# RWKV pair loop of a two-layer encoder: front work spread over two steps, one factor by 32x32 transposes, eight conditioning steps moved

## The chip, the cores and the metric

The kernel is written instruction by instruction for one core of a Trainium2 chip. Each engine (TensorE = PE, VectorE = DVE, ScalarE = ACT, GpSimd = POOL, SyncE = SP) runs its own list of instructions in order, and an instruction may wait for semaphores that others raise. The metric is the device time of one execution in microseconds; of several runs the median is given.

## What is computed

The reference is a two-layer encoder on a sequence of 256 tokens of width 2048, in fp32. Every sub-layer is `x <- LayerNorm(alpha*x + (1+gate) * f(x*(1+scale)+shift))`, with shift, scale and gate from a conditioning vector c. Layer 0 mixes tokens with a bidirectional RWKV-7 scan (16 heads of 64) beside gated linear attention (GLA, 4 heads); layer 1 with differential attention; each layer has a SwiGLU FFN behind it. The change is in the RWKV part and in where layer 0's conditioning is computed:

```
def _ada(c, w, b):                       # shift, scale, gate of one sub-layer
    mod = silu(c) @ w + b
def step(S, inp):                        # RWKV-7, forward and backward in time
    r_t, w_t, k_t, v_t, kk_t, a_t = inp
    sa = -einsum('dbhvk,dbhk->dbhv', S, kk_t)
    S = (S * w_t[..., None, :] + sa[..., :, None] * (kk_t * a_t)[..., None, :]
         + v_t[..., :, None] * k_t[..., None, :])
    return S, einsum('dbhvk,dbhk->dbhv', S, r_t)
```

with `kk = l2norm(k * k_k)`, `k = k * (1 + (a-1) * k_a)`, `w = exp(-0.607 * sigmoid(...))`, and to the output of the scan a normalisation per head, a bonus `sum(r*k*r_k) * v` and a gate g.

## The kernel before

The matrix products with large weights run as three fp32r matmuls for each tile (high and low parts). The RWKV scan between the input projection and the output projection is done in chunks of 64 tokens: 4 chunks, 2 directions, so 8 units of 64x64 for each head; two heads make a pair (one on partitions 0 to 63, one on 64 to 127), and there are 8 pairs. Inside a chunk the recurrence is a triangular system, and its inverse is built up in levels: blocks of 1, 2, 4, ... 32 columns are merged. The kernel holds it twice, as V and as its transpose W. At level lv the PE forms `L1 = GA^T V` (`level_q`, 16 matmuls of 64x64, two for each unit), the DVE masks it to Q, the PE forms `V += W^T Q` in bank L2 (`level_v`) and `W += Q^T W` in bank L3 (`level_w`), and ACT copies both banks to R_V and R_W. At level 5 only W is formed, and copied to R_WF.

A loop over t runs from -2 to 8 and works on three pairs at a time:

- levels of pair t (`lev`): five `level_q`, four `level_v`, five `level_w`; the second half of its masked scores (`scores(t,2)`, `scores(t,3)`); transposes of its factors (`turn_ab`, `turn_v`);
- chain of pair c = t-1 (`chain`): for chunk i the PE does `chain_x`, ACT copies R_X, the PE does `chain_u` (L2361 for all of these), ACT copies R_U (L1489), the PE does `chain_s`, the DVE updates the state (`state`, L1949, L1952); then `outputs(c)`, its moments on the DVE, the normalisation a step later;
- front of pair n = t+1 (`front`): the token shift (`shifts`, `mix`), running sums of the decay (`sums`), the norm of k (`square` on ACT, `head_sums` on the PE, `clamp` on the DVE, then `norm_ln` L1439 and `norm_exp` L1444 on ACT, each behind a table load), `exps` (L1453), `keys`, `unit_keys` (L1894 to L1899, which raises q_ready), `factors` (L1909 to L1915), then `scores(n,0)`, `scores(n,1)`, their masks (L1924) and `first(n)` (L1930, L1935 on the DVE, then on the PE 16 transposes into L2 and 16 copies into L3) with which the levels start, and `bonus(n)` (L2558). The z columns of pair t+2 are turned (`z_turn`, L2378) and multiplied for the decays (`up_decays`, L2387) at the end of the step.

The order is written out by hand, as one loop body for each engine; nothing reorders it. Steps t = -2 and -1 fill this pipeline, step 7 also begins GLA (`gla = t == PAIRS - 1`), and step 8 has pair 7's chain beside GLA.

The conditioning of a part is 16 steps `cond_step(u)` of the DVE, each a multiply-add over 128x2048 (L526) of a 1 MB piece of ada_w that SP has fetched to one of two slots of adaw. Units u = 32 to 47 run in the loop, two in each of the steps 0 to 7, and SP fetches them in a loop of its own ahead of the weights of the output projection. GLA uses the same slots for its own work after that. The output projection has 16 units (q, s): for each, ACT rounds 1 MB of weights (`high`), the DVE takes the remainder (`low`, L479), the PE does 24 matmuls; at s = 2 of q = 1, 2, 3 the DVE also does `end_block`.

Of the kernel before, what the change touches and what calls it, by code (L numbers as in the profile page):

```python
# [14 lines left out]
P = 128  # L15
# [4 lines left out]
W = 512  # L20
# [82 lines left out]
def build_trunk(nc, x_in, c_in, ada_w, ada_b, ln_g, ln_b, ffn_w_in, ffn_w_out, ab_w_in, ab_w_out,  # L103
# [3 lines left out]
    with ExitStack() as ctx:  # L107
# [59 lines left out]
        R_v = sb("R_v", [P, 2, SEQ], stack=r2)  # L167
        R_sq = sb("R_sq", [P, SEQ], stack=r2)
# [24 lines left out]
        R_bonus = sb("R_bonus", [P, 3, SEQ], stack=r2)  # L193
        R_g = sb("R_g", [P, 4, SEQ], stack=r2)
        R_dec = sb("R_dec", [P, 3, NCH, 2], stack=r2)
# [105 lines left out]
        JOBS = (0, 1, 4, 5)  # L301
        FIRST_JOBS = len(JOBS) + 1
# [63 lines left out]
        wc_ready = sem("wc_ready")  # L366
# [856 lines left out]
        def _(sp):  # L1223
# [23 lines left out]
            for u in range(32, 48):  # L1247
                if u == 45:
# [100 lines left out]
        def _(act):  # L1349
# [69 lines left out]
            def rates(n):  # L1419
# [4 lines left out]
                if n > 3:  # L1424
                    act.wait_ge(tail_done, n - 3)
                act.activation(R_lw[:, 2], P1[:, 0:SEQ], ACT.Sigmoid, bias=tab[:, T_A0 + n:T_A0 + n + 1])
                act.activation(R_g[:, n % 4], P1[:, SEQ:W], ACT.Copy).then_inc(up_act, 1)

            def square(n):
# [4 lines left out]
                act.activation(R_sq[:], R_rk[:, 1], ACT.Square, scale=neg[:, n:n + 1]).then_inc(sq_ready, 1)  # L1434
# [11 lines left out]
            def exps(n):  # L1446
# [4 lines left out]
                if n > 2:  # L1451
                    act.wait_ge(s_ready, 3 * (n - 2))
# [3 lines left out]
                act.activation(R_dec[:, n % 3, :, 0], e1_at[:, 0, :, CH - 1], ACT.Copy)  # L1456
                act.activation(R_dec[:, n % 3, ::-1, 1], e1_at[:, 1, :, 0], ACT.Copy).then_inc(exps_ready, 1)
# [18 lines left out]
            def level_w(t, lv):  # L1476

                act.wait_ge(w_done, 5 * t + lv)
                act.activation(flat(R_WF if lv == LEVELS - 1 else R_W), L3, ACT.Copy).then_inc(wc_ready, 1)
# [81 lines left out]
            for t in range(-2, PAIRS + 1):  # L1561
                c, n, m = t - 1, t + 1, t + 2
                lev, chain, front = 0 <= t < PAIRS, 0 <= c < PAIRS, 0 <= n < PAIRS
                if chain:
                    chain_x(c, 0)
                if t == PAIRS - 1:
                    gla_gate_act()
# [9 lines left out]
                if front:  # L1577
                    rates(n)
                    if m < PAIRS:
                        load_up(m)  # L1580
                if lev:
                    level_w(t, 1)
                if t == PAIRS - 1:
                    out_gate(0)
                if front:
                    square(n)
# [6 lines left out]
                if t == PAIRS - 1:  # L1593
                    out_gate(1)
                if t == PAIRS:
                    gla_exps(1)
                if lev:
                    level_w(t, 2)
                if front:
                    norm_ln(n)  # L1600
                if chain:
                    chain_x(c, 2)
                if lev:
# [5 lines left out]
                if front:  # L1609
                    norm_exp(n)  # L1610
                if lev:
                    level_w(t, 3)
                if t == PAIRS - 1:
                    gla_exp(0)
                    gla_exp(1)
                if front:
                    exps(n)
                if chain:
                    chain_x(c, 3)
                if lev and t < PAIRS - 1:  # L1620
                    turned_ab(t, 0)
                if lev:
                    level_v(t, 4)
                if t == PAIRS - 1:
# [4 lines left out]
                if lev and t < PAIRS - 1:  # L1629
                    turned_ab(t, 1)  # L1630
                if lev:
                    level_w(t, 4)
                if t == PAIRS - 1:
                    turned_ab(t, 0)
                if lev:
                    turned_v(t)
                if t == PAIRS - 1:
                    turned_ab(t, 1)
                if lev:
                    level_w(t, 5)  # L1640
                if t == PAIRS - 1:
# [3 lines left out]
                if t == PAIRS:  # L1645
                    gla_exps(2)
                if chain:
# [3 lines left out]
                if m < PAIRS:  # L1651
                    z_copy(m)
                if front:
                    level_v(n, 0)
                if m < PAIRS:
                    z_own(m)
                    decays(m)
# [132 lines left out]
        def _(dve):  # L1790
# [66 lines left out]
            def mix(n):  # L1857
# [3 lines left out]
                if n > 1:  # L1861
                    dve.wait_ge(v_turned, n - 1)
                for j in (1, 0, 2):
                    o = R_rk[:, j] if j < 2 else R_v[:, n % 2]
# [62 lines left out]
            def first(n):  # L1927
# [5 lines left out]
                if n:  # L1933
                    dve.wait_ge(w_done, 5 * n)
                dve.tensor_tensor(R_W[:], R_C0[:], eye2.unsqueeze(1).to_broadcast((P, NU, CH)), ALU.add).then_inc(first_ready, 1)  # L1935
# [6 lines left out]

            def state(c, i):

                dec = R_dec[:, c % 3, i].unsqueeze(2).to_broadcast((P, 2, CH))
# [8 lines left out]
            def bonus(n):  # L1954

                dve.wait_ge(bonus_done, n + 1)
                dve.tensor_tensor(R_bonus[:, n % 3], C2[:, SEQ:W], R_v[:, n % 2], ALU.mult).then_inc(bonus_out, 1)
# [955 lines left out]
```

## Time and profile before

| what | us |
|---|---|
| median of 3 runs (2801.75 to 2805.22) | 2802.12 |
| the profiled execution, whole | 2806.61 |
| its span | 2804.8 |
| PE busy over the span | 2638.8 (94%) |
| DVE / ACT busy over the span | 1978.6 (71%) / 1149.2 (41%) |
| loop from the first z_turn (t = -2) to the end of step 6 | 387.76 to 638.92 |
| step 7 and step 8 with the rest of GLA | 638.92 to 733.55 |

The span is the profiled execution's from first to last instruction. A "step" of the loop is counted from the first matmul of its `level_q(t,1)` to that of the next. Steps 1 to 5 repeat with 33.1 to 33.4 us each; the one shown in the rows is t = 4, at 539.85 to 573.22. A busy time of the PE counts the length of each matmul, and these overlap; what a block of matmuls costs is the distance from its start to the start of the next block, when nothing waits between them.

### The profile page before, as it was taken

What the parts mean: (1) busy time and instruction counts of PE and PEld (TensorE: products, weight loads), DVE (VectorE), ACT (ScalarE), POOL (GpSimd) and SP (SyncE); (2) the same over time, 40 slices, a digit from 0 to 9 for tenths busy, and PEclk for the clock granted to TensorE, in tenths of its full rate; (3) what the DMA queues carried; (4) which work ended last, traced back from release to release, by engine and by line L of the source; (5) the groups of instructions that cost most, each with busy time, mean ns of one, the idle gap of its engine ahead of it and who ended that gap; (6) DMA issues with size and microseconds to landing.
All of it is one profiled execution on the core that took longest, in us unless ns stands there. A gap on an engine that the chain in (4) does not pass through costs nothing. (4 is left out here: it accounts for less than half of the span.)

```text
span 2804.8 us, 42833 instructions
## 1 busy us (share of the span) xinstructions
PE 2638.8 (94%) x18094; PEld 2197.3 (78%) x18094; DVE 1978.6 (71%) x1855; ACT 1149.2 (41%) x1319; POOL 283.8 (10%) x199
## 2 busy tenths in 40 slices
PE   1999979998899999999999899999999999999996
PEld 1888869997777888888888677888778888888885
DVE  6778956776566878888888778865668755555557
ACT  1443335555434333333333345546443333333332
POOL 0000000000004000000000086541040000000000
PEclk9999989999999999999999899999999999999998
DMA  9999912220546888888888467744568755555552
GB/s 352 330 337 368 372 65 72 72 68 32 210 152 240 328 298 329 302 327 303 325 307 323 134 211 251 271 155 140 189 222 316 270 185 191 194 186 188 194 189 81
DMA packets 252890, 636.73 MB, mean 227 GB/s; under 512 B 10222, under 2 KB 17060, under 8 KB 230596
## 3 DMA queue, kind: packets, MB, share of 16 engines
q1 hardware_dynamic: 246578, 621.84, 62.2%
q10 hardware_dynamic: 6162, 12.72, 1.2%
q8 instruction: 115, 1.88, 0.3%
q14 instruction: 35, 0.29, 0.0%
HBM read 632.42 MB, written 2.10 MB: 226 GB/s over the span
## 5 line engine op out<-in xcount | busy, mean ns | idle before, releaser
L479 DVE TENSOR_TENSOR s_wl<-s_raw,s_wh 128x2048 fp32r<-128x2048 f32 x393 | 913.7, 2325 | 509.4 <-ACT s_wh L474 501.1
L474 ACT ACTIVATE s_wh<-s_raw 128x2048 fp32r<-128x2048 f32 x396 | 758.3, 1915 | 1163.6 <-PE pa L639 503.0
L637 PE MATMUL pa<-s_wh,s_hth 128*128 128x512 f32 x1616 | 646.0, 400 | 17.2 <-DVE s_wl L479 11.4
L639 PE MATMUL pa<-s_wh,s_htl 128*128 128x512 f32 x1616 | 635.0, 393 | 0.0
L638 PE MATMUL pa<-s_wl,s_hth 128*128 128x512 f32 x1616 | 634.6, 393 | 0.0
L637 PEld LDWEIGHTS pa<-s_wh,s_hth 128*128 128x128 f32 x1616 | 307.0, 190 | 92.6 <-DVE s_wl L479 16.1
L639 PEld LDWEIGHTS pa<-s_wh,s_htl 128*128 128x128 f32 x1616 | 306.6, 190 | 65.5
L526 DVE SCALAR_TENSOR_TENSOR s_wide<-s_adaw,s_silu_c,s_wide 128x2048 f32<-128x2048 f32 x150 | 351.8, 2346 | 6.4 <-DMA s_adaw<-in_ada_w 6.4
L638 PEld LDWEIGHTS pa<-s_wl,s_hth 128*128 128x128 f32 x1616 | 307.1, 190 | 60.2
L637 PE MATMUL pb<-s_wh,s_hth 128*128 128x512 f32 (+1 forms) x816 | 318.9, 391 | 0.7 <-DVE s_wl L479 0.7
L639 PE MATMUL pb<-s_wh,s_htl 128*128 128x512 f32 (+1 forms) x816 | 318.6, 390 | 0.0
L638 PE MATMUL pb<-s_wl,s_hth 128*128 128x512 f32 (+1 forms) x816 | 318.6, 390 | 0.0
L637 PE MATMUL py<-s_wh,s_guh 128*128 128x512 f32 x640 | 251.2, 393 | 4.4 <-DVE s_ysum L1061 4.4
L639 PE MATMUL py<-s_wh,s_gul 128*128 128x512 f32 x640 | 249.3, 390 | 0.0
L638 PE MATMUL py<-s_wl,s_guh 128*128 128x512 f32 x640 | 249.1, 389 | 0.0
L637 PEld LDWEIGHTS pb<-s_wh,s_hth 128*128 128x128 f32 x816 | 154.0, 189 | 33.7 <-DVE s_wl L479 1.9
L639 PEld LDWEIGHTS pb<-s_wh,s_htl 128*128 128x128 f32 x816 | 154.0, 189 | 31.8
L638 PEld LDWEIGHTS pb<-s_wl,s_hth 128*128 128x128 f32 x816 | 154.0, 189 | 31.5
L876 POOL TENSOR_TENSOR s_small<-s_small 128x2 f32<-128x2 f32 x4 | 3.8, 947 | 1585.0 <-DVE s_small L865 1585.0
L1061 DVE TENSOR_TENSOR s_ysum<-s_ysum,py 128x512 f32<-128x512 f32 x172 | 116.4, 683 | 47.3 <-PE py L639 46.9
L637 PEld LDWEIGHTS py<-s_wh,s_guh 128*128 128x128 f32 x640 | 120.1, 188 | 35.2 <-DVE s_ysum L1061 7.7
L639 PEld LDWEIGHTS py<-s_wh,s_gul 128*128 128x128 f32 x640 | 120.1, 188 | 25.3
(372 smaller groups left out, 2698.2 us busy)
## 6 DMA issues: line engine op xcount, KB each, us to landing
s_raw<-in_ffn_w_in SPq DMA_DIRECT2D x176, 1024.0 KB, 5.2
s_adaw<-in_ada_w SPq DMA_DIRECT2D x160, 1024.0 KB, 6.0
s_raw<-in_ffn_w_out SPq DMA_DIRECT2D x88, 1024.0 KB, 7.5
s_raw<-in_ab_w_in SPq DMA_DIRECT2D x48, 1024.0 KB, 9.0
s_raw<-in_diff_w_in SPq DMA_DIRECT2D x48, 1024.0 KB, 5.2
s_raw<-in_ada_w SPq DMA_DIRECT2D x16, 1024.0 KB, 8.5
s_raw<-in_ab_w_out SPq DMA_DIRECT2D x16, 1024.0 KB, 5.4
s_qkv<-in_ada_w SPq DMA_DIRECT2D x16, 1024.0 KB, 7.2
```

The source lines that it names most:

```text
L474: act.activation(wh[:, s % 2, :, 0:width], raw[:, s, :, 0:width], ACT.Copy).then_inc(hi_done, 1)
L479: dve.tensor_tensor(wl[:, s % 2, :, 0:width], raw[:, s, :, 0:width], wh[:, s % 2, :, 0:width].bitcast(F32), ALU.subtract).then_inc(lo_done, 1)
L526: dve.scalar_tensor_tensor(wide[:], frm, silu_c[:, bass.ds(k, 1)], wide[:], ALU.mult, ALU.add).then_inc(ada_step, 1)
L637: pe.matmul(o, a_hi, w_hi, start=start and k == 0, stop=False)
L638: pe.matmul(o, a_hi, w_lo, start=False, stop=False)
L639: mm = pe.matmul(o, a_lo, w_hi, start=False, stop=stop and k == UK - 1)
L876: pool.tensor_tensor(small[:, 38:40], small[:, 34:36], small[:, 95:96].to_broadcast((P, NT)), ALU.pow).then_inc(end_rstd, 1)
L1061: dve.tensor_tensor(y, y, py[:, i], ALU.add).then_inc(py_free, 1)
```

## The change

- The loop runs from t = -3. The front of a pair is split: z_turn, z_copy, z_own, decays now work on pair q = t+3; up_rates, rates, shifts, mix, sums, square, head_sums, clamp, keys, norm_ln, norm_exp, exps, unit_keys, bonus on pair m = t+2 (`ahead`); factors, scores(n,0), scores(n,1), their masks, first and level_v(n,0) on n = t+1 (`front`). R_v, R_bonus, R_g and R_dec have one buffer more, and R_sq is gone (R_rn takes its place).
- `level_w` of levels 1 to 4, ACT's copies of R_W (`level_w`) and the second half of `first` are gone. In their place the DVE turns R_V to R_W in blocks of 32x32 (`level_t`, four in each step); up to level 4 the units are zero outside such blocks. Level 5 remains as `last_w`, for which ACT writes R_W into bank L3 ahead (`last_seed`).
- Units 40 to 47 of the conditioning move to eight units of the output projection (`OUT_STEPS`), DVE step and fetch both; the loop has one cond_step in each step, and SP waits for the end of GLA (`head_done`) ahead of fetch 40.

The diff, cut to this:

```diff
+        OUT_STEPS = ((1, 0), (1, 1), (1, 3), (2, 0), (2, 1), (2, 3), (3, 0), (3, 1))
...
@@ def out_sp
                     load_unit(sp, c0 + q, s, wv[s, :, :, q * W:(q + 1) * W])
+                    if (q, s) in OUT_STEPS:
+                        u = 40 + OUT_STEPS.index((q, s))
+                        if u == 40:
+                            sp.wait_ge(head_done, GH)
+                        load_part(sp, u, u % 2, parts[1, 1, u - 32])
@@ def out_dve
+                    if (q, s) in OUT_STEPS:
+                        cond_step(dve, 40 + OUT_STEPS.index((q, s)))
@@ sync
-            for u in range(32, 48):
+            for u in range(32, 40):
@@ scalar, loop
+                if ahead:
+                    norm_ln(m)
...
+                if lev and not gla:
+                    turned_v(t)
+                if lev:
+                    last_seed(t)
...
+                if front:
+                    level_v(n, 0)
+                if ahead:
+                    norm_exp(m)
                 if lev:
-                    level_w(t, 4)
...
+                    last_w(t)
...
+                if ahead:
+                    exps(m)
@@ vector
+            def level_t(t, lv):
+
+                dve.wait_ge(vc_ready, 5 * t + lv + 1)
+                dve.transpose(flat(R_W), flat(R_V)).then_inc(wt_ready, 1)
...
                 if front:
                     masked(n, 0)
                     masked(n, 1)
                     first(n)
                 if lev and not gla:
-                    cond_step(dve, 32 + 2 * t)
+                    cond_step(dve, 32 + t)
+                if lev:
+                    level_t(t, 4)
+                    level_q(t, 5)
...
+                if ahead:
+                    unit_keys(m)
+                    bonus(m)
...
-                if lev and not gla:
-                    cond_step(dve, 33 + 2 * t)
@@ tensor
                 if lev:
                     level_q(t, 5)
                 if front:
-                    scores(n, 0)
-                    scores(n, 1)
+                    first(n)
+                if chain:
+                    outputs(c)
                 if lev:
-                    level_w(t, 5)
+                    last_w(t)
...
-                if chain:
-                    outputs(c)
-                if front:
-                    bonus(n)
-                if m < PAIRS:
-                    z_turn(m)
-                    up_decays(m)
-                if front:
-                    first(n)
+                if ahead:
+                    bonus(m)
+                if q < PAIRS:
+                    z_turn(q)
+                    up_decays(q)
```

ACT, in the middle of step 3 before: the second table load (L1444) and the exponential that ends the norm of k stand behind the copy R_U of chunk 2, ahead of chunk 3's R_X.

```order
L1489 ACTIVATE s_R_U<-pb 128x2x64
L1444 ACT_TABLE_LOAD
L1444 ACTIVATE s_R_rn<-s_R_rn 128x256
L1479 ACTIVATE s_R_W<-pa 128x512
L1453 ACTIVATE s_R_e<-s_R_cs 128x8x64
L1454 ACTIVATE s_R_e<-s_R_cs 128x512
```

ACT, end of a step after: chunk 3's copies (L1498 would be R_X, L1503 is R_U), then R_VV, the seed of L3 (L1488), R_V of `first(n)`, and only then that table load (L1453).

```order
L1503 ACTIVATE s_R_U<-pb 128x128
L1478 ACTIVATE s_R_VV<-py 128x256
L1488 ACTIVATE pa<-s_R_W 128x512
L1483 ACTIVATE s_R_V<-pt 128x512
L1453 ACT_TABLE_LOAD
L1453 ACTIVATE s_R_rn<-s_R_rn 128x256
L1493 ACTIVATE s_R_WF<-pa 128x512
L1462 ACTIVATE s_R_e<-s_R_cs 128x8x64
```

The exponential has moved behind two copies that wait for the end of the step: the seed for the fourth transpose, R_V for `first(n)` on the PE.

DVE, end of step 3 before: unit_keys (L1894 to L1899) and factors come ahead of the masks of the scores; cond_step (L526) follows first.

```order
L1899 TENSOR_TENSOR s_R_qa<-s_R_kk,s_R_lw 128x256
L1909 TENSOR_TENSOR s_raw<-s_R_kk,s_R_e 128x8x64
L1910 TENSOR_TENSOR s_raw<-s_R_rk,s_R_e 128x8x64
L1913 TENSOR_TENSOR s_xt<-s_R_ks,s_R_e 128x8x64
L1915 TENSOR_TENSOR s_xt<-s_R_qa,s_R_e 128x8x64
L1940 TENSOR_TENSOR s_R_Q<-py,s_cst 128x512
L1924 TENSOR_TENSOR s_raw<-pt,s_cst 128x512
L1924 TENSOR_TENSOR s_raw<-pa,s_cst 128x512
L1930 TENSOR_TENSOR s_R_C<-s_raw,s_cst 128x512
L1935 TENSOR_TENSOR s_R_W<-s_R_C,s_cst 128x512
L526 SCALAR_TENSOR_TENSOR s_wide<-s_adaw,s_silu_c,s_wide 128x2048
L1957 TENSOR_TENSOR s_R_bonus<-pb,s_R_v 128x256
```

The same place after: masks, first, cond_step (L528), the fourth transpose (L1952), the mask of level 5 (L1946), and then unit_keys (L1902 to L1907).

```order
L1932 TENSOR_TENSOR s_raw<-pt,s_cst 128x512
L1932 TENSOR_TENSOR s_raw<-pa,s_cst 128x512
L1938 TENSOR_TENSOR s_R_C<-s_raw,s_cst 128x512
L1941 TENSOR_TENSOR s_R_C<-s_R_C,s_cst 128x512
L528 SCALAR_TENSOR_TENSOR s_wide<-s_adaw,s_silu_c,s_wide 128x2048
L1952 STREAM_TRANSPOSE s_R_W<-s_R_V 128x512
L1946 TENSOR_TENSOR s_R_Q<-py,s_cst 128x512
L1902 SCALAR_TENSOR_TENSOR s_R_kk<-s_R_rk,s_neg,s_R_rn 128x256
L1905 SCALAR_TENSOR_TENSOR s_R_rkr<-s_R_rk,s_tab,s_R_ks 128x256
L1907 TENSOR_TENSOR s_R_qa<-s_R_kk,s_R_lw 128x256
L1968 TENSOR_TENSOR s_R_bonus<-pb,s_R_v 128x256
```

The cond_step and the fourth transpose now stand between first and unit_keys, whose last instruction raises q_ready.

PE, end of step 3 before, from the last products of outputs(c) to the next step's `level_q`: bonus (L2558), z_turn, up_decays, and `first` in two halves.

```order
L2361 MATMUL pb<-s_R_S,s_raw 64x64 x2
L2558 MATMUL pb<-s_R_rkr,s_cst 128x256
L2378 MATMUL py<-s_cst,s_z 128x128 x4
L2378 MATMUL pt<-s_cst,s_z 128x128 x2
L2387 MATMUL pa<-s_raw 128x256 x2
L2361 MATMUL pt<-s_cst,s_R_W 64x64 x16
L2361 MATMUL pa<-s_R_W,s_cst 64x64 x16
L2361 MATMUL py<-s_R_V,s_raw 64x64 x16
```

After: last_w behind outputs(c), then bonus (L2570, which waits for q_ready), z_turn, up_decays, and the next `level_q`.

```order
L2373 MATMUL pb<-s_R_S,s_raw 64x64 x2
L2373 MATMUL pa<-s_R_W,s_R_Q 64x64 x16
L2570 MATMUL pb<-s_R_rkr,s_cst 128x256
L2391 MATMUL py<-s_cst,s_z 128x128 x4
L2391 MATMUL pt<-s_cst,s_z 128x128 x2
L2402 MATMUL pa<-s_raw 128x256 x2
L2373 MATMUL py<-s_R_V,s_raw 64x64 x16
```

`first` has moved ahead of outputs(c), last_w behind it, and nothing but bonus, z_turn and up_decays is left between last_w and the next step.

## Rows read from the trace of the kernel before

**Rows 1.** Page, busy time of each engine over the span

```profile
PE 2638.8 (94%) x18094; PEld 2197.3 (78%) x18094; DVE 1978.6 (71%) x1855; ACT 1149.2 (41%) x1319; POOL 283.8 (10%) x199
```

**Rows 2.** Stages: length, busy PE, PEld, DVE, ACT, POOL; PEclk, DMA share, GB/s

```profile
387.76:412.19 24.43, 14.98 (x126) 11.56 (x128) 11.58 (x21) 10.29 (x22) 0.00 (x0) 0.59 0.05 16
412.19:440.06 27.87, 26.01 (x682) 24.24 (x680) 18.05 (x30) 16.86 (x33) 0.00 (x0) 1.00 0.08 17
539.85:573.22 33.37, 32.76 (x922) 31.16 (x920) 24.58 (x51) 18.82 (x42) 3.07 (x2) 1.00 0.24 75
606.90:638.92 32.02, 31.41 (x918) 29.97 (x916) 23.23 (x50) 17.89 (x40) 1.93 (x1) 1.00 0.19 60
638.92:679.53 40.61, 34.30 (x832) 31.43 (x829) 27.55 (x44) 19.65 (x33) 3.07 (x1) 0.92 0.14 52
733.55:824.00 90.45, 88.65 (x405) 73.43 (x404) 49.03 (x39) 38.57 (x35) 0.89 (x2) 0.99 0.65 222
```

**Rows 3.** Timeline of PE in step 4: start, length, instruction, idle before

```profile
541.11 0.70 PE L2393 MATMUL py<-s_raw 96*128 96x256 f32 x2
...
542.61 1.15 PE L2361 MATMUL pt<-s_R_Q,s_R_W 64*64 64x64 f32 x32
543.59 0.40 PE L2361 MATMUL pb<-s_R_X,s_R_WF 64*64 64x64 f32 x8
543.82 1.10 PE L2361 MATMUL pa<-s_R_W,s_R_Q 64*64 64x64 f32 x32
544.75 0.29 PE L2361 MATMUL pb<-s_R_VV,s_R_AT 64*64 64x64 f32 x4
...
546.10 1.10 PE L2361 MATMUL py<-s_R_V,s_raw 64*64 64x64 f32 x32
...
564.69 1.04 PE L2361 MATMUL pa<-s_raw,s_xt 64*64 64x128 f32 x16
...
569.16 0.70 PE L2558 MATMUL pb<-s_R_rkr,s_cst 128*128 128x256 f32 x2
...
571.31 1.15 PE L2361 MATMUL pt<-s_cst,s_R_W 64*64 64x64 f32 x32
...
573.22 0.98 PE L2361 MATMUL py<-s_R_V,s_raw 64*64 64x64 f32 x28
```

**Rows 4.** Timeline of DVE in step 4

```profile
547.24 0.69 DVE L1940 TENSOR_TENSOR s_R_Q<-py,s_cst 128x512 f32<-128x512 f32 x1 [0.62 <-PE py L2361]
...
567.33 0.69 DVE L1935 TENSOR_TENSOR s_R_W<-s_R_C,s_cst 128x512 f32<-128x512 f32 x1
567.93 2.35 DVE L526 SCALAR_TENSOR_TENSOR s_wide<-s_adaw,s_silu_c,s_wide 128x2048 f32<-128x2048 f32 x1
```

**Rows 5.** Timeline of ACT in step 4

```profile
543.80 0.60 ACT L1474 ACTIVATE s_R_V<-pt 128x512 f32<-128x512 f32 x1 [0.67 <-PE pt L2361]
...
544.29 0.27 ACT L1489 ACTIVATE s_R_U<-pb 128x128 f32<-128x128 f32 x1
...
556.44 1.28 ACT L1444 ACT_TABLE_LOAD   x1
557.74 0.42 ACT L1444 ACTIVATE s_R_rn<-s_R_rn 128x256 f32<-128x256 f32 x1
```

**Rows 6.** Groups by line on DVE: the transposes of 32x32 blocks elsewhere

```profile
L559 DVE STREAM_TRANSPOSE s_qkv<-s_wide 128x1024 f32<-128x1024 f32 x4 | 4.9, 1230 | 0.0
```

**Rows 7.** Timeline of DVE while the pipeline fills

```profile
400.25 0.48 DVE L1894 SCALAR_TENSOR_TENSOR s_R_kk<-s_R_rk,s_neg,s_R_rn 128x256 f32<-128x256 f32 x1 [1.42 <-ACT s_R_rn L1444]
...
401.20 0.43 DVE L1899 TENSOR_TENSOR s_R_qa<-s_R_kk,s_R_lw 128x256 f32<-128x256 f32 x1
```

**Rows 8.** Two long waits of PE in step 8 (timeline)

```profile
707.70 1.80 PE L2627 MATMUL pt<-s_z,s_L_kdt 64*128 64x256 f32 x8 [1.92 <-ACT s_L_kdt L1532]
...
730.94 1.91 PE L2649 MATMUL pb<-s_adaw,s_L_qb 128*64 128x256 f32 x12 [2.44 <-DVEq L2049]
```

**Rows 9.** PE behind the first of them: length, busy, PEclk, DMA share, GB/s

```profile
708.00:708.50 0.50, 0.50 (x6) 0.54 0.00 0
...
711.00:711.50 0.50, 0.50 (x9) 0.54 0.00 0
```

More of the change, by code:

```diff
@@ L1474, in level_v, with last_seed, last_w @@
                 act.activation(flat(R_V), L2, ACT.Copy).then_inc(vc_ready, 1)
-            def level_w(t, lv):
-                act.wait_ge(w_done, 5 * t + lv)
-                act.activation(flat(R_WF if lv == LEVELS - 1 else R_W), L3, ACT.Copy).then_inc(wc_ready, 1)
+            def last_seed(t):
+                act.wait_ge(wt_ready, 4 * t + 4)
+                act.activation(L3, flat(R_W), ACT.Copy).then_inc(ws_ready, 1)
+            def last_w(t):
+                act.wait_ge(w_done, t + 1)
+                act.activation(flat(R_WF), L3, ACT.Copy).then_inc(wf_ready, 1)
             def chain_x(c, i):
@@ L1560, in _ @@
             load_up(0)
[L1561 to L1563 removed]
+            for t in range(-3, PAIRS + 1):
+                c, n, m, q = t - 1, t + 1, t + 2, t + 3
+                lev, chain, front, ahead = 0 <= t < PAIRS, 0 <= c < PAIRS, 0 <= n < PAIRS, 0 <= m < PAIRS
+                gla = t == PAIRS - 1
                 if chain:
                     chain_x(c, 0)
[L1566 removed]
+                if gla:
                     gla_gate_act()
@@ L2077, in _ @@
                 if front:
-                    shifts(n)
-                    mix(n)
+                    factors(n)
+                if ahead:
+                    shifts(m)
                 if chain:
                     state(c, 0)
-                if tail and not gla:
+                if lev:
+                    level_t(t, 1)
+                    level_q(t, 2)
+                if ahead:
+                    mix(m)
+                if 0 <= p and not gla:
                     normed(p)
-                if lev:
-                    level_q(t, 2)
                 if gla:
@@ L2461, in turn_v @@
                 for k in range(NCH):
-                    mm = two(unit(P1, k), R_v[:, t % 2, k * CH:(k + 1) * CH], eye2, start=(k == 0))
+                    mm = two(unit(P1, k), R_v[:, t % 3, k * CH:(k + 1) * CH], eye2, start=(k == 0))
                 mm.then_inc(v_turned, 1)
@@ L2470, in first @@
                 for u in range(NU):
-                    mm = two(unit(L2, u), R_W[:, u], eye2, start=(u == 0))
+                    mm = two(unit(L2, u), R_C0[:, u], eye2, start=(u == 0))
                 mm.then_inc(v_done, 1)
-                if n:
-                    pe.wait_ge(wc_ready, 5 * n)
-                for u in range(NU):
-                    two(unit(L3, u), eye2, R_W[:, u], start=(u == 0))
             def level_q(t, lv):
@@ L2664, in gla_turn_out @@
                 mm.then_inc(g_oT, 1)
-            for t in range(-2, PAIRS + 1):
+            for t in range(-3, PAIRS + 1):
+                c, n, m, q = t - 1, t + 1, t + 2, t + 3
+                lev, chain, front, ahead = 0 <= t < PAIRS, 0 <= c < PAIRS, 0 <= n < PAIRS, 0 <= m < PAIRS
                 gla = t == PAIRS - 1
-                c, n, m = t - 1, t + 1, t + 2
-                lev, chain, front = 0 <= t < PAIRS, 0 <= c < PAIRS, 0 <= n < PAIRS
                 if lev:
@@ L2677, in _ @@
                     gla_turn(2)
-                if front:
-                    up_rates(n)
+                if ahead:
+                    up_rates(m)
                 if lev:
@@ L2699, in _ @@
                     chain_x(c, 1)
-                if n >= 0 and not gla:
-                    head_sums(n, t - 2)
                 if lev:
@@ L2710, in _ @@
                     pe.wait_ge(g_logit, 3)
-                    head_sums(n, t - 2)
+                    head_sums(m, t - 2)
                 if chain:
                     chain_s(c, 1)
+                if m >= 0 and not gla:
+                    head_sums(m, t - 2)
                 if lev and not gla:
```

212 lines of the change are left out of this document (93 added, 119 removed).

## The prediction

> **What bounds the kernel now.** I read the engines' busy time first. TensorE works 2638.8 of 2804.8 us [rows 1], so over the whole the other engines are cover. That is an average over stages, so the windows come next [rows 2]: step 4 of the loop lasts 33.37 us with TensorE busy for 32.76, at full clock; DVE has 24.6 and ACT 18.8. In the out-projection TensorE is busy for 88.65 of 90.45 us. Only the filling of the pipeline (15.0 busy of 24.4, clock 0.59) and step 7 (34.3 of 40.6) have TensorE waiting. Third, the timelines of step 4 on three engines give what the change turns on: how far apart blocks of matmuls start, and how long a result takes on its way through DVE or ACT and back [rows 3 to 5]. The bound in the loop is TensorE's own work. The question is whether it still is once a seventh of that work is gone.
>
> **What goes from TensorE.** A level_w costs 0.93 (543.82 to 544.75 in [rows 3]); the two halves of `first` cost 1.91 (571.31 to 573.22), half of that 0.96. The step loses 4 x 0.93 + 0.96 = 4.68 us. It has 33.37 - 0.8 of waits and gaps = 32.6 of work, so 27.9 is left. Seven steps (0 to 6) lose this, step 7 loses the four level_w.
>
> **What TensorE then waits for, in a full step.** I laid the new orders of PE, ACT and DVE beside each other with the durations of before.
> - *Chain.* Between `chain_u` and `chain_s` stood a level_w, which covered ACT. From the start of chain_u (543.59) its copy R_U is ready at 544.29 + 0.27 = 544.56, with some 0.06 to start the matmuls; but ACT copies R_V first (543.80, 0.60), and chain_u is now issued right behind level_v. From level_v's start (542.61) R_V's copy comes 1.19 later, R_U's 0.49 behind that, and 0.33 ends it: chain_s starts 2.01 behind level_v, where level_v and chain_u take 0.98 + 0.23 = 1.21. That is 0.80 of wait, three times in a step: 2.4.
> - *Mask.* level_q to Q takes 1.14 (546.10 to 547.24 in [rows 3, 4]) and 0.69 more. At level 2 only 1.3 us of other work is left in between: 0.5 of wait. At the other levels scores, turn_ab and chain blocks cover it.
> - *`first`.* scores(n,1) start at 564.69, and the mask for the transposes is ready at 567.33 + 0.69 = 568.02, 3.33 later [rows 3, 4]. Before, outputs, bonus and z_turn lay in between. Now it is scores(n,1) itself (0.88) and level_q(t,5) (0.93): 1.6 of wait (3.33 + 0.06 - 1.81). The wait for factors (0.6) ahead of scores goes in return; it is in the 0.8 above.
> - *The 32x32 transposes.* No such transpose of 128x512 is in the trace. The nearest row has 128x1024 at 1.23 [rows 6], so 0.62 by proportion, and from below 0.3, from above 1.23. I take 0.69, as DVE's other operations over 128x512 take [rows 4]. Three of them lie beside chain and scores. Level_q needs R_V and not R_W; level_v needs both Q and R_W, so transposes are late only by their own length. At 1.23 each step would be 1 to 2 us longer, at 0.3 none.
> - *bonus(m).* This is the place that decides. It waits for q_ready, raised by the last of unit_keys. Those wait for norm_exp, which on ACT now stands behind last_seed and R_V of `first`; and on DVE they stand behind cond_step, the fourth transpose and Q of level 5. Count from F, the start of scores(n,1). DVE: masks and first until F + 3.24, cond_step until + 5.49 (2.25, its 2.35 less 0.1 of overlap [rows 4]), transpose until + 6.18. ACT, released by that transpose: last_seed 0.5, R_V of `first` 0.62, until + 7.30; table load 1.28 and the exponential 0.42 [rows 5], beginning at + 8.6, Q-norm ready at + 9.0; unit_keys take 1.38 with the first matmul behind them (400.25 to 401.63, [rows 7]): + 10.4, and 0.1 of semaphores, F + 10.55. TensorE: scores, level_q, the wait and 0.98 of transposes until + 4.4, outputs 2.66 (566.50 to 569.16), last_w 0.93: F + 7.96. **The wait is 2.6 us.** DVE, not the table load alone, is half of it: without cond_step in the way the wait would be near 0.4.
> - The rest (exps behind it, the copies of rates, GpSimd) has ten microseconds until it is read, and I cost it at nothing.
>
> Sum of a full step: 27.9 + 2.4 + 0.5 + 1.6 + 2.6 = **35.0 us, against 33.37: +1.6.** The busy share falls to 0.8, and the bound moves to the loop through ACT and DVE.
>
> **By stretches.** Step 0 has no chain to wait for but the bonus wait: 27.87 to 28.6, +0.7. Steps 1 to 4: +6.5. Step 5 has the bonus wait but no z_turn and up_decays any more (1.6, from 569.69 to 571.31 [rows 3]): 0. Step 6 has no `ahead`: up_rates (1.5, 541.11 to 542.61), head_sums (1.2, two blocks of 0.6) and bonus (0.53) have moved one step up, and with the 4.68 taken and some 4 of waits added 32.0 becomes 28.7: -3.3. Step 7, where TensorE waits on DVE [rows 2], has one conditioning step less (2.25) ahead of the masks of GLA, and no level_w: -4.0 for steps 7 and 8. *Filling:* the first level_q comes at 412.19 now. One more step is walked through, whose chain is norm, table load, scores of pair 0 and then that of pair 1; laid out with the durations of the filling of before, at TensorE's half clock, it comes at 424.8: **+12.6**. *Out-projection:* each unit has 90.45/16 = 5.65 us for TensorE, and DVE is busy 49.0 of 90.45; so it idles for 41, in which eight steps of 2.25 (18 us) fit, in units without an end_block: 0, with +2 as upper end. 8 MB are fetched besides, at a DMA share of 0.65. The fetches stand on SP's queue behind the weights of their unit, and the first waits there for GLA's end, with unit (1,1)'s weights behind it; GLA is over by then.
> Sum: 12.6 + 0.7 + 6.5 + 0 - 3.3 - 4.0 + 0 = **+12.5.**
>
> **The clock.** Behind two waits of TensorE in step 8, of 1.92 and 2.44 us [rows 8], the granted clock fell to 0.50, the lower of its two levels (1.2 GHz); for the first the 3.50 us that followed ran at 0.51 [rows 9], which loses 3.5 x 0.49 = 1.7 us. After waits up to 0.8 in the loop it stayed at 1.00 [rows 2]. The bonus wait of 2.6 stands in six steps (0 to 5), directly behind work at full pace. I count four falls: 4 x 1.65 = +6.6. In all 12.5 + 6.6 = +19, on the profiled 2806.6. I put it on the median, 4.5 below: 2802.1 + 19 = **2821**.
>
> ACT's table load takes 1.28 here and its exponential starts 1.30 behind the load's start [rows 5]. The Trainium skill, "ScalarE: Activation LUTs", section on what a table load costs, gives about 1283 ns and another 1380 ns of drain for each switch, 2.66 us. By the trace the second part is not there; by the page the bonus wait would be 1.4 longer in seven places, some +10 us (an estimate from the page). The row decides.
>
> **Rivals.**
> - *The clock stays.* The waits are 2.6 beside 1.6 and six of 0.8, and one wait of 1.42 in step 7 brought no fall at once. Then +12.5: 2814.6. Chance 0.20.
> - *The clock falls more often* (with `first`'s 1.6 and the bonus wait 5 us later, in all six steps, or twice), or the transposes take their upper end: 6 x 1.65 x 1.3 or 5 x 1.5 in place of 6.6, 2825 to 2831. Chance 0.20.
> - *The out-projection gets late.* If DVE's remainder of the weights waited for cond_step, up to 8 x 2.25 = 18 more, 2824 to 2839. Against it stands DVE's idle time there. Chance 0.05.
> - *No bonus wait.* If norm_exp came in time (ACT's sequence reaches it ahead of R_V of `first`, or DVE has cond_step done sooner since its slot's data is early), six waits of 2.6 go, with their clock: 2821 - 15.6 - 6.6 = 2799, which is within 0.2%. Chance 0.07.
> - *The other side: TensorE stays the bound.* Then all 4.68 comes back in seven steps (-32.8), step 7 gives 4, and the filling costs 12.6 (less if it overlaps better): -24, 2778. It decides by whether R_U's copy and the masks come within the work left: my waits of 0.8 and 1.6 would have to be covered, so ACT would have to be 0.8 faster between level_v and chain_s than in [rows 5]. Nothing speaks for it but that I may have placed the blocks wrongly. Partly so (half the waits) gives 2795. Chance 0.10, all of it faster.
>
> **How the numbers follow.** The forecast has 0.38, its own range 2810 to 2829. With the rivals above and below 2802 to 2833 leaves out 0.10 + 0.07 below and some 0.03 above. A change of 0.2%, 5.6 us, is what a measurement of this kernel can just tell from none: same is 2796.5 to 2807.7. Faster 0.10, same 0.07, slower 0.83.
>
> **What would show it.** Right: first level_q(0,1) near 425; steps 1 to 4 of 35 us; in them TensorE idle ahead of bonus (L2570) for 2.4 to 2.6 released by DVE's L1907, ahead of `first` 1.6 released by DVE's L1941, ahead of chain_s three times 0.8 released by ACT's L1503; DVE's L1952 at 0.6 to 0.7; stretches at PEclk 0.50 behind bonus; the out-projection at 90 to 92. Wrong: steps of 29 us with TensorE busy throughout; L1952 above 1 us; a clock at 1.00 through steps 1 to 5, or lower in all of them; DVE late with low in the out-projection.

## The result: 38 us slower by the medians, twice what was forecast

| | before | after |
|---|---|---|
| median of 4 runs, us | 2801.93 | 2839.70 |
| all runs, us | 2800.99 to 2805.22 | 2834.24 to 2840.53 |
| ratio | 1 | 1.0126 (95%: 1.0114 to 1.0138) |
| span of the profiled execution, us | 2804.8 | 2838.4 |

The direction was forecast, the size was not: 2821 with a range of 2802 to 2833, and 2839.7 measured. Measured again with the run wt_best below, the changed kernel gave 1.0124 (1.0109 to 1.0140). The spans of the two profiled executions lie 33.6 us apart; the working below is against that. "Lower clock" in the table is what the lower granted clock lost: for each half microsecond one minus the granted clock, times the time that TensorE was busy in it.

The stages of the kernel after, in the columns of [rows 2] (length, busy PE, PEld, DVE, ACT, POOL, then PEclk, DMA share, GB/s): filling, step 0, step 3, step 6, steps 7 and 8, and the out-projection with its end:

```profile
387.12:427.49 40.37, 25.17 (x115) 18.16 (x115) 17.90 (x34) 20.73 (x42) 0.00 (x0) 0.50 0.06 16
427.49:458.34 30.85, 24.13 (x517) 21.69 (x516) 19.62 (x33) 15.20 (x30) 0.00 (x0) 0.89 0.14 45
529.92:566.59 36.67, 30.54 (x758) 27.89 (x757) 25.02 (x54) 18.00 (x42) 2.02 (x2) 0.96 0.12 39
637.41:668.26 30.85, 26.12 (x737) 25.32 (x738) 19.15 (x41) 6.72 (x18) 1.01 (x1) 0.94 0.01 3
668.26:766.47 98.21, 76.95 (x1157) 64.03 (x1153) 62.96 (x146) 47.64 (x114) 7.39 (x9) 0.84 0.13 44
766.47:862.74 96.27, 94.37 (x422) 77.93 (x421) 69.22 (x50) 38.98 (x33) 0.89 (x2) 0.97 0.81 306
```

The kernel before in the two stages that [rows 2] cut differently (steps 7 and 8 together, out-projection with its end):

```profile
638.92:733.55 94.63, 77.63 (x1284) 64.76 (x1281) 64.03 (x136) 48.02 (x115) 9.46 (x9) 0.90 0.19 67
733.55:827.98 94.43, 92.63 (x422) 76.69 (x421) 51.10 (x42) 39.15 (x35) 0.89 (x2) 0.99 0.65 223
```

| stage | before | after | difference | lower clock, before and after | forecast, clock apart |
|---|---|---|---|---|---|
| filling (first z_turn to first level_q) | 24.4 | 40.4 | +15.9 | 5.3, 12.4 | +12.6, at half clock |
| step 0 | 27.9 | 30.9 | +3.0 | 0, 2.6 | +0.7 |
| steps 1 to 4 | 133.2 | 144.5 | +11.4 | 0, 4.2 | +6.5 |
| steps 5 and 6 | 65.7 | 65.4 | -0.3 | 0, 2.6 | -3.3 |
| steps 7 and 8 | 94.6 | 98.2 | +3.6 | 8.9, 12.6 | -4.0 |
| out-projection and its end | 94.4 | 96.3 | +1.8 | 0.9, 2.7 | 0 |
| all else | | | -1.8 | | 0 |
| sum | | | +33.6 | +15.0 without the filling | +12.5, and 6.6 of clock |

In the loop TensorE is no longer full: busy 30.5 of 36.7 us in step 3, where [rows 2] have 32.8 of 33.4. Where it waits is read from the timeline of PE (start, length, instruction, idle before and its releaser), step 3 of the kernel after:

```profile
534.84 0.33 PE L2373 MATMUL pb<-s_R_VV,s_R_AT 64*64 64x64 f32 x4 [0.72 <-ACT s_R_U L1503]
...
538.11 1.15 PE L2373 MATMUL pt<-s_R_Q,s_R_W 64*64 64x64 f32 x32 [0.32 <-DVE s_R_Q L1946]
539.09 0.40 PE L2373 MATMUL pb<-s_R_X,s_R_WF 64*64 64x64 f32 x8
540.12 0.33 PE L2373 MATMUL pb<-s_R_VV,s_R_AT 64*64 64x64 f32 x4 [0.63 <-ACT s_R_U L1503]
...
547.05 0.33 PE L2373 MATMUL pb<-s_R_VV,s_R_AT 64*64 64x64 f32 x4 [0.63 <-ACT s_R_U L1503]
...
553.34 1.13 PE L2373 MATMUL py<-s_R_V,s_raw 64*64 64x64 f32 x32
555.87 1.15 PE L2373 MATMUL pt<-s_cst,s_R_C 64*64 64x64 f32 x32 [1.41 <-DVE s_R_C L1941]
...
559.48 1.15 PE L2373 MATMUL pa<-s_R_W,s_R_Q 64*64 64x64 f32 x32
563.05 0.70 PE L2570 MATMUL pb<-s_R_rkr,s_cst 128*128 128x256 f32 x2 [2.42 <-DVE s_R_qa L1907]
```

These are the six waits of the prediction, at their places and by their releasers. The idle time printed is a little shorter than what a wait costs, since the matmul before it is drawn to its very end (0.40 where the next would start after 0.23). By starts: 540.12 - 539.09 - 0.23 = 0.80 ahead of chain_s; 555.87 - 553.34 - 0.93 = 1.60 ahead of `first`; 563.05 - 559.48 - 0.93 = 2.64 ahead of bonus. The chain behind the last is read from DVE and ACT in the same step:

```profile
555.73 2.35 DVE L528 SCALAR_TENSOR_TENSOR s_wide<-s_adaw,s_silu_c,s_wide 128x2048 f32<-128x2048 f32 x1
558.00 0.70 DVE L1952 STREAM_TRANSPOSE s_R_W<-s_R_V 128x512 f32<-128x512 f32 x1
...
561.61 0.49 DVE L1902 SCALAR_TENSOR_TENSOR s_R_kk<-s_R_rk,s_neg,s_R_rn 128x256 f32<-128x256 f32 x1 [2.34 <-ACT s_R_rn L1453]
```

```profile
558.73 0.60 ACT L1488 ACTIVATE pa<-s_R_W 128x512 f32<-128x512 f32 x1 [5.23 <-DVE s_R_W L1952]
559.27 0.58 ACT L1483 ACTIVATE s_R_V<-pt 128x512 f32<-128x512 f32 x1
559.87 1.28 ACT L1453 ACT_TABLE_LOAD   x1
561.16 0.42 ACT L1453 ACTIVATE s_R_rn<-s_R_rn 128x256 f32<-128x256 f32 x1
```

ACT stood still for 5.23 us for the fourth transpose, which stood behind the conditioning step; only then came the seed, R_V, the table load and the exponential for which unit_keys waited.

The clock, from windows of PE (length, busy, PEclk, DMA share, GB/s) at the waits for bonus that end at 527.77, 563.05 and 599.94, all 2.42 long; the first window begins inside its wait:

```profile
526.50:530.50 4.00, 2.73 (x31) 1.00 0.11 43
563.50:567.50 4.00, 4.00 (x34) 0.57 0.01 4
601.00:605.00 4.00, 4.00 (x48) 0.57 0.07 20
```

Twice the granted clock fell to its lower level (1.2 GHz), which loses 4.0 x 0.43 = 1.7 us, and once, behind the same wait, it did not. From step 0 to 6 the falls lose 9.4 us in the kernel after and nothing in the kernel before. Without them steps 1 to 4 are 34.7 to 35.2 us long, 35.1 on average where 35.0 was forecast.

### The profile page after: what moved, and what is told of

It reads as the page before. It is cut to its first block and busy times, and to the rows that moved or that the text cites. A ratio compares the mean times of both kernels' runs of the same rounds, so it can differ in the third digit from the quotient of the medians.

```text
span 2838.4 us, 40259 instructions
## 1 busy us (share of the span) xinstructions
PE 2626.9 (93%) x16814; PEld 2178.6 (77%) x16814; DVE 1998.6 (70%) x1887; ACT 1136.8 (40%) x1295; POOL 272.0 (10%) x199
## 5 line engine op out<-in xcount | busy, mean ns | idle before, releaser
L528 DVE SCALAR_TENSOR_TENSOR s_wide<-s_adaw,s_silu_c,s_wide 128x2048 f32<-128x2048 f32 x150 | 351.8, 2346 | 0.0
L639 PEld LDWEIGHTS py<-s_wh,s_guh 128*128 128x128 f32 x640 | 120.1, 188 | 35.2 <-DVE s_ysum L1070 7.7
```

What stands on the lines that cost most here:

```text
L528: dve.scalar_tensor_tensor(wide[:], frm, silu_c[:, bass.ds(k, 1)], wide[:], ALU.mult, ALU.add).then_inc(ada_step, 1)
L639: pe.matmul(o, a_hi, w_hi, start=start and k == 0, stop=False)
```

## Experiments

All ratios are to the kernel before, timed in the same rounds on the same chip.

**The moved conditioning alone (cond_only).** The kernel before with

```diff
-            for u in range(32, 48):
+            for u in range(32, 40):
...
                     load_unit(sp, c0 + q, s, wv[s, :, :, q * W:(q + 1) * W])
+                    if (q, s) in OUT_STEPS:
+                        u = 40 + OUT_STEPS.index((q, s))
+                        if u == 40:
+                            sp.wait_ge(head_done, GH)
+                        load_part(sp, u, u % 2, parts[1, 1, u - 32])
...
+                        cond_step(dve, 40 + OUT_STEPS.index((q, s)))
```

and one conditioning step in each step of the loop.

> The kernel before with one part of the change alone: conditioning units 40 to 47 computed and fetched in the output projection, one conditioning step for each step of the loop. Theory A (this part is nearly free, the loss lies in the loop's waits and in the filling): steps 0 to 5 unchanged, step 7 shorter by up to 2, the output projection longer by the 1.8 us seen in the changed kernel: 2799 to 2805. Theory B (the time beyond my forecast lies here, because DVE or the fetches are late in the output projection): 2808 to 2815.

Measured: 0.9996 (0.9987 to 1.0005). Steps 1 to 5 last 32.9 to 33.4, the out-projection and its end 93.9. (By the same rows these steps last 32.9 to 33.7 in the kernel before, not 33.1 to 33.4.) Steps 7 and 8 last 91.0 for 94.6 in these two profiles, 2.5 of that by fewer falls of the clock; in the time of all runs no gain is clear. This part costs nothing; theory B falls.

**W by transposes, without the split front (wt_cond).** The loop order of the kernel before; `level_w` 1 to 4 out on PE and ACT, `level_t` ahead of each next `level_q` on DVE, `last_seed` in the place of ACT's copy of level 4.

> The changed kernel without the front split: the loop order of the kernel before, W by 32x32 transposes, conditioning moved. Theory A (removing level_w gives TensorE time back except where it covered ACT's copy of U; the split front is what costs, by the wait ahead of bonus and a longer filling): a step loses 4.7 of work and gains about 3 of waits, no wait ahead of bonus, filling as before: 7 steps of about -1.7, 2788 to 2794. Theory B (the transposes on DVE are on the path, whatever the front does): steps as long as in the changed kernel without its bonus wait, 2802 to 2812.

Measured: 2798.1, 0.9975 (0.9965 to 0.9986), 7 us less than the kernel before. That is less than theory A gave (8 to 14), and a step shows why: 33.18 us, 0.2 less than before with 4.7 of work gone. (Steps 7 and 8 last 90.0, 4.7 less than before.) The stage, and all waits of PE in it (in total, times, longest):

```profile
536.05:569.23 33.18, 29.17 (x756) 26.91 (x756) 24.75 (x53) 17.49 (x39) 1.01 (x1) 1.00 0.13 42
```

```profile
PE pb L2373 <- ACT s_R_U L1504: 2.0, 3, 0.7
PE py L2373 <- ACT s_R_V L1484: 1.2, 2, 0.7
PE pt L2373 <- DVE s_xt L1924: 0.9, 1, 0.9
```

No engine is full: DVE has 24.8 and ACT 17.5 of 33.2. The work that was taken out had covered the time that results take through other engines. The printed waits are 4.1 in all where the step before has 0.6, and each costs a little more than is printed, so together they are about as long as the work was.

**unit_keys ahead (a_keys).** The changed kernel with

```diff
@@ ACT
+                if ahead:
+                    norm_exp(m)
                 if lev:
                     last_seed(t)
...
-                if ahead:
-                    norm_exp(m)
@@ DVE
-                if lev and not gla:
-                    cond_step(dve, 32 + t)
...
                     unit_keys(m)
+                if lev and not gla:
+                    cond_step(dve, 32 + t)
+                if ahead:
                     bonus(m)
```

> The changed kernel with two moves: on ACT norm_exp (table load and exponential) ahead of last_seed instead of behind R_V of first, on DVE the conditioning step between unit_keys and the product with bonus instead of ahead of the fourth transpose. Theory A (the wait ahead of bonus comes from that chain, and TensorE's clock falls behind it): 2.4 us less in each of steps 0 to 5 and the falls of the clock in steps 1 to 5 gone (1.7 each), 2815 to 2819. Theory B (another wait takes its place, or the clock falls for another reason): only the wait or part of it goes, 2824 to 2832.

Measured: 2819.3, 1.0049 (1.0035 to 1.0063), where the changed kernel has 1.0126 and 1.0124: 21 us less. The wait for bonus is gone and steps 1 to 5 run at full clock. The steps are 33.5 and not 32.4, because another wait has come up, 0.8 ahead of up_rates for ACT's z_own, behind exps. The first row is the whole step, the others all waits of PE in it:

```profile
514.73:548.24 33.51, 29.03 (x758) 26.84 (x757) 24.75 (x53) 17.24 (x39) 1.01 (x1) 1.00 0.14 43
```

```profile
PE pb L2374 <- ACT s_R_U L1503: 2.0, 3, 0.7
PE pt L2374 <- DVE s_R_C L1941: 1.4, 1, 1.4
PE py L2409 <- ACT s_R_zo L1415: 0.8, 1, 0.8
PE pt L2374 <- DVE s_R_Q L1946: 0.3, 1, 0.3
```

**The wait filled with work (a_fill).** Nothing gets shorter here; TensorE turns the same columns three more times while it waits; with `False` the turn raises no semaphore.

```diff
+                if lev and q < PAIRS:
+                    for extra in range(3):
+                        z_turn(q, False)
                 if ahead:
                     bonus(m)
```

> The changed kernel with three further z_turn of the coming pair in each of steps 0 to 4 ahead of bonus, whose results are overwritten by the real one: 2 us of TensorE work inside its wait of 2.4, nothing shortened. Theory A (the lower clock follows the wait): the time falls by 1.7 for each of the falls behind bonus, 4 or 5 of them, 2831 to 2834, with steps of 35.0. Theory B (the clock falls for the sum of waits in the step or something else): 2839 to 2842, the falls stay.

Measured: 2828.5, 1.0085 (1.0071 to 1.0099), 11 us less than the changed kernel with 10 us more of work for TensorE. One of its steps:

```profile
490.56:525.83 35.27, 31.26 (x776) 28.90 (x775) 24.85 (x53) 17.17 (x40) 1.02 (x1) 1.00 0.13 40
```

Steps 1 to 5 stand at PEclk 1.00 though the smaller waits are still there, so those of 0.3 to 1.4 us bring no fall there by themselves: the wait for bonus is needed. (In step 0 the fall stays, shorter, behind waits of 1.4.) That the wait for bonus is enough is not shown; a_chain below speaks against it. Steps 0 to 6 are 6.4 us shorter, 6.2 of it by the clock; in the profile the rest lies in the filling and in steps 7 and 8, which the edit does not touch and where the clock stood otherwise in this execution (37.7 for 40.4, and 94.4 for 98.2). So only some 6 of the 11 us are shown to come from the edit.

**Step 8 put back (a_step8).** Reading steps 7 and 8 after the result, I found a move that no term of my sum had. In step 8 `head_sums` (the transposes of pair 6's normalised outputs) stood ahead of chunk 1's chain_u before, behind its chain_s after. The kernel after, PE and then DVE:

```profile
715.81 0.69 PE L2373 MATMUL pb<-s_R_X,s_R_WF 64*64 64x64 f32 x8 [3.90 <-ACT s_R_X L1498]
...
717.78 1.06 PE L2373 MATMUL pa<-s_cst,s_R_yn 64*64 64x64 f32 x16
...
722.37 0.69 PE L2373 MATMUL pb<-s_R_S,s_raw 64*64 64x64 f32 x8 [3.10 <-DVE s_R_S L1963]
```

```profile
718.89 0.48 DVE L1992 SCALAR_TENSOR_TENSOR s_R_bonus<-pa,s_tab,s_R_bonus 128x256 f32<-128x256 f32 x1 [6.21 <-PE pa L2373]
...
721.67 0.28 DVE L1960 TENSOR_TENSOR s_R_S<-s_R_S,pb 128x128 f32<-128x128 f32 x1
```

DVE's `finish` waits 6.21 for those transposes, and behind it stand three products of GLA (0.69 each) and the state for which TensorE then waits 3.10. Before, they took the time in which TensorE waited for R_X anyway:

```profile
684.89 0.68 PE L2361 MATMUL pa<-s_cst,s_R_yn 64*64 64x64 f32 x16 [1.71 <-DVE s_R_yn L1974]
686.93 0.45 PE L2361 MATMUL pb<-s_R_X,s_R_WF 64*64 64x64 f32 x8 [1.36 <-ACT s_R_X L1484]
```

```diff
+                if t == PAIRS:
+                    head_sums(m, t - 2)
                 if lev:
                     level_v(t, 2)
...
-                if m >= 0 and not gla:
+                if m >= 0 and t < PAIRS - 1:
                     head_sums(m, t - 2)
```

> The changed kernel with one block of TensorE put back: in step 8 the transposes of the normalised outputs of pair 6 (head_sums) stand ahead of chunk 1's chain_u again, as before the change, instead of behind its chain_s. Theory A (this move, which no term of my sum had, makes DVE's finish wait 6.2 us and the state of chunk 1 3.1 us late): steps 7 and 8 fall from 98.2 to 93 to 95, 3 to 5 us less than the changed kernel, about 2836 where the kernel before has 2805. Theory B (steps 7 and 8 are long for the clock alone): within 1 us of the changed kernel.

Measured: 2832.6, 1.0107 (1.0089 to 1.0125), 5 us less than the changed kernel. The intervals overlap, so the time alone does not show it. The profile does: steps 7 and 8 take 89.6 us, for 98.2 and 97.5 in the two profiles of the changed kernel. Their row, and the stretch of lower clock at the place of the waits in the changed kernel (714 to 728) and in a_step8 (709 to 716):

```profile
665.21:754.78 89.57, 70.67 (x1158) 58.73 (x1154) 62.77 (x146) 47.33 (x114) 7.14 (x9) 0.94 0.14 49
```

```profile
714.00:728.00 14.00, 8.34 (x100) 0.52 0.01 1
709.00:716.00 7.00, 5.56 (x56) 0.51 0.01 2
```

Of the 8.6 us between the profiles 7.5 are lower clock (12.6 and 5.1 lost) and 1.1 is the rest; against the second profile it is 5.5 of 7.9. So the moved block costs mostly by the clock. How much of the clock belongs to the move is not settled by one profile; over all profiles, steps 7 and 8 take 94.4 to 99.8 in the five where head_sums stands late in step 8, and 89.6 to 92.7 in the six changed versions where it stands early.

**chain_u ahead of level_v (a_chain).** On PE and ACT, in steps 0 to 6:

```diff
+                if chain and t < PAIRS - 1:
+                    chain_u(c, 1)
                 if lev:
                     level_v(t, 2)
-                if chain:
+                if chain and t >= PAIRS - 1:
                     chain_u(c, 1)
```

so for all four chunks, and `scores(t, 3)` moved between chain_x(c,1) and chain_u(c,1).

> The changed kernel with chain_u ahead of level_v, on TensorE and on ACT, in steps 0 to 6, and scores(t,3) between chain_x(c,1) and chain_u(c,1) so that R_X is ready. Theory A (chain_s waits since level_w no longer covers ACT's copy of U; level_v can cover it): the three waits of 0.8 go, 2.5 in each of steps 1 to 6, -15 against the changed kernel, 2823 to 2829. Theory B (R_V and with it level_q and the transposes get late by as much): -5 at most, 2835 to 2841.

Measured: 2825.5, 1.0077 (1.0062 to 1.0092), 13 us less than the changed kernel, near theory A. None of the three waits for R_U is left. The two full steps without a fall are 33.7 and 34.3, some 1.4 and 0.8 shorter and not 2.5, because a wait comes up for `finish`, which now is late for turn_ab, and in these two steps one of 0.3 and 0.8 for R_X besides. Steps 0 to 6 are 15 us shorter, 4.4 of it by fewer falls. All six waits for bonus are still 2.42 long, and only three falls came at them (at 453.5, 488.0 and 522.0) and none in steps 3 to 6: that wait alone does not decide. The waits of PE in step 2:

```profile
PE pb L2578 <- DVE s_R_qa L1915: 2.4, 1, 2.4
PE pt L2381 <- DVE s_R_C L1949: 1.4, 1, 1.4
PE pa L2381 <- DVE s_xt L2003: 0.9, 1, 0.9
```

**All of it on the split front (best1).** a_keys, a_step8 and a_chain together; exps on ACT right behind norm_exp; outputs(c) ahead of first(n) on PE, its copy ahead of R_V on ACT.

> The changed kernel with all: norm_exp and exps ahead of last_seed on ACT, conditioning step behind unit_keys, chain_u ahead of level_v, outputs(c) ahead of first(n), output copy ahead of R_V of first, step 8 as before. Theory A (the split front pays once the waits are covered): steps of 28.6 to 29.5 in place of 33.4, filling 11 to 12 longer than before, 2778 to 2792. Theory B (DVE or ACT bound the step near 31 to 32 or the clock falls again): 2795 to 2806.

Measured: 2788.0, 0.9944 (0.9930 to 0.9959), within theory A. Steps 2 to 4 last 30.1 us, 0.6 above what was expected; the filling is still 34.8 and the whole 14 us faster than before, 50 us faster than the changed kernel.

**The same on the front of before (wt_chain, wt_best).** First wt_cond with chain_u ahead of level_v and first(n) ahead of bonus:

> W by transposes and the moved conditioning with the front of the kernel before (run wt_cond, steps of 33.18), with chain_u ahead of level_v and first(n) ahead of bonus. Theory A (what ate the 4.7 us of removed work is waits of an in-order engine that other work can cover: 2.5 for U, 0.9 for R_V of first): steps of 29.8 to 30.5, 2772 to 2782. Theory B (the front's chain through ACT and DVE to factors binds the step at 33): 2792 to 2799, TensorE waiting 3 us more for factors.

Measured: 2788.3, 0.9942 (0.9929 to 0.9955), steps of 30.5 to 31.1. That lies between the two theories, 6 us above A's range (2772 to 2782). The steps come near A's 29.8 to 30.5, and the front's chain does not bind at 33 as B had it. Its filling rose to 27.5, since first(n) now stood ahead of z_turn there too, at the lower clock. Then

```diff
@@ ACT
                 if chain:
                     chain_x(c, 0)
+                if front:
+                    decays(n)
...
                     z_own(m)
-                    decays(m)
@@ PE
-                if front:
+                if front and lev:
                     first(n)
...
                     up_decays(m)
+                if front and not lev:
+                    first(n)
```

> Run wt_chain with two moves: ACT's decays (table load and two sigmoids, 2.1 us) behind its copy of R_X of chunk 0 instead of ahead of it, and first(n) behind up_decays while the pipeline fills, as in the kernel before. Theory A (what is left in the step is ACT's order again): the wait of 0.8 ahead of chain_u(c,0) goes in six steps, the filling returns from 27.5 to 24.4: 2778 to 2783. Theory B (decays are then late for up_rates and rates): the step stays at 30.6 or grows, 2785 to 2790.

Measured: 2780.2, 0.9916 (0.9902 to 0.9929). A step, the filling, and all waits of PE in the step:

```profile
497.39:527.25 29.86, 28.43 (x757) 26.60 (x757) 24.76 (x53) 17.82 (x40) 1.01 (x1) 1.00 0.15 49
387.15:412.40 25.25, 15.30 (x94) 11.49 (x95) 11.58 (x21) 10.21 (x22) 0.00 (x0) 0.56 0.05 15
```

```profile
PE pb L2384 <- ACT s_R_X L1499: 0.7, 1, 0.7
PE py L2384 <- ACT s_R_V L1484: 0.7, 1, 0.7
```

This is the fastest version found, 24 us below the kernel before and some 59 below the changed one, as theory A had it. It has the transposes and the moved conditioning, and not the split front.

**The changed kernel again (after_again).**

> The changed kernel once more, on the chip of the next run. By the first measurement it is 1.26% longer than the kernel before: 2836 to 2842 where that has 2802 to 2805. If where TensorE's clock falls varies between executions, its runs spread by more than those of the kernel before (up to 6 us), with one fall (1.7 us) more or less at a time.

Measured: 2838.9, 1.0124 (1.0109 to 1.0140), four runs from 2837.2 to 2840.5, no wider apart than those of the kernel before in the same rounds (2800.9 to 2807.1). Its steps 0 to 5 agree with the first profile within 0.05 us, but the fall in step 6 is gone (29.2 for 30.9), and its out-projection with its end is 94.21 and not 96.27:

```profile
764.10:858.31 94.21, 92.45 (x423) 76.47 (x422) 69.21 (x50) 39.20 (x35) 0.89 (x2) 0.99 0.83 312
```

So the 1.8 us of the first profile are no cost of the conditioning steps. There a wait for DVE's `low` was followed by a fall, and the kernel before has about the same wait without one. PE in the first profile of the kernel after (the matmul with its wait; the window behind it), then in the kernel before:

```profile
781.82 0.47 PE L639 MATMUL pa<-s_wh,s_hth 128*128 128x512 f32 x1 [1.90 <-DVE s_wl L481]
...
784.00:788.00 4.00, 4.00 (x16) 0.80 1.03 423
```

```profile
748.72 0.47 PE L637 MATMUL pa<-s_wh,s_hth 128*128 128x512 f32 x1 [1.80 <-DVE s_wl L479]
...
748.50:752.00 3.50, 3.28 (x15) 1.00 0.99 419
```

## Why the prediction was wrong in size

- **The step: right.** Each wait was where and as long as I had it (three of 0.8, 0.5, 1.6, 2.6), the transpose of 128x512 took 0.70 for the 0.69 assumed, and the mean step without its falls lasts 35.1 for 35.0. a_keys shows the chain behind the wait for bonus, a_chain that of U. The Trainium skill, "ScalarE: Activation LUTs", section on what a table load costs, adds 1380 ns of drain for each switch of tables. That is not seen here either: the exponential starts 1.29 behind the load's start (559.87 to 561.16).
- **Steps 7 and 8: the failed step, 7.6 us.** "One conditioning step less ahead of the masks of GLA, and no level_w: -4.0" took what the diff removes there and left out what it moves; it came out at +3.6. The removals alone do give that: wt_cond, with both of them and the old order, has 90.0 us there for 94.6. head_sums changed its place in step 8, and my order rows were of step 3 only. With it put back (a_step8) the two steps take 89.6. Of the 7.6 us, 3.8 are lower clock, which I had counted nowhere behind step 5 although the kernel before already loses 8.9 to it in these steps. A second thing is in that term: a step that is bound by waits gets shorter by less than the work taken out of TensorE, as I had read from [rows 2] for step 7 myself. The four level_w are 3.7 us of work, and from cond_only to wt_cond the two steps shrink by 1.0 (2.2 with the clock taken out).
- **The filling: the term mis-sized, 3.3 us.** The first level_q came at 427.5 and not at 424.8, and the filling began 0.6 sooner. The chain was right (norm, table load, scores, the next pair), but the last table load stood behind the copy of `first`: TensorE did `first` at 417.8, R_V's copy came at 419.8, and bonus waited 3.84 for unit_keys until 423.6. a_keys, which takes the table load out from behind that copy, has a filling of 36.4.
- **The clock: the term mis-sized, 8.4 us.** I counted four falls of 1.65, 6.6 us. Outside the filling the lower clock loses 15.0 more than before: 9.4 in steps 0 to 6, 3.8 more in steps 7 and 8, 1.8 more in the out-projection. In steps 0 to 5 there were four falls, as I had counted; no row gave that number, so this was luck. The first of them lasts 7 us and loses 2.6, and it came behind waits of 1.38 and 1.39 and not at bonus; a fifth came in step 6. That those of steps 1 to 5 need the wait for bonus was right (a_fill).
- **Sum.** Clock apart, the filling is 3.3 above the forecast, steps 0 to 6 are 0.7 above it, steps 7 and 8 3.8, and all else is 1.8 below: 6.0. With 8.4 of clock this makes up the 14.5 between 19.1 and 33.6. The medians lie another 4 us apart, since the profiled execution of before was 4.7 above its median; I had put the whole forecast on that median without room for it. One sum was off in itself: the terms of step 6 give 28.1 and not 28.7; without its fall it took 29.1.
- **The rivals.** "The clock falls more often" came nearest. The out-projection did not get late, as cond_only shows. "TensorE stays the bound" was wrong as it stood, and yet it named the right quantity: with the waits covered (wt_best) steps 2, 3 and 5 are 29.9 us.
- **What I didn't ask.** The forecast compared the change as it stands. wt_cond shows that taking out 4.7 us for each step gave 0.2 back in itself, in an order written for the old lengths. The split of the front, whose filling costs 10 to 16 us once, was not needed for the gain: the versions with and without it have steps of 30.1 and 29.9.

What stays open: why the clock falls behind some waits of 2.42 us and not behind others. The Trainium skill, "TensorE: Matmul & The Clock Gate", section on what is actually happening, says that where the clock changes varies from run to run, with a phase that does not start with the kernel. The traces agree only in part. From step 6 on, the two profiles of the changed kernel differ: a fall at 642 in one and not in the other. But in steps 0 to 5 three profiles (both of the changed kernel, and a_step8, which is the same up to step 8) have their falls at the same places, behind the waits for bonus of steps 1, 3 and 4 and not behind those of steps 2 and 5. No run here can set that phase, nor tell what made these places repeat.

## What to carry to other kernels

In an in-order engine a block of work can also be the cover for a latency elsewhere. Before taking it out, list what it covered, and move another block into its place in the same change: the same removal gave 0.2 us for each step as it was and 3.5 with chain_u ahead of level_v and two neighbours moved. Look for moves in every stage of the loop, its first and last steps above all: the order of a middle step doesn't show them. And keep slow steps of a side job (here a conditioning step of 2.3 us and a table load) behind whatever raises the next semaphore for the full engine.

## What the hardware showed that I had not expected

- With 2 us of useless matmuls in each of five waits (2.42 us in four of them) the kernel was 11 us faster (a_fill against the changed kernel), 6 of them in the loop by the clock alone; the other 5 are not shown to come from the edit.
- A wait of 3.90 and one of 3.10 us, 6.6 apart, went with 14 us at the lower clock (PEclk 0.52 from 714 to 728); with waits of 1.71, 0.74 and 0.33 in their place it was 7 us (a_step8).
- The 32x32 transposes of 128x512 fp32 take 0.70 us each on DVE and start the next instruction after 0.62, like its other operations over 128x512 (0.69 in [rows 4]), and stay hidden in both best versions.
- The fetches of the out-projection went from 223 to 312 GB/s (0.65 to 0.83 of the DMA engines), and its time stayed the same (94.43, and 94.21 in after_again).
